# Grouped attention of a two-block kernel, turned from queries on partitions to keys on partitions

## The reference, cut to what matters

```python
def gqa_attention(q, k, v, q_norm, k_norm):
    q = apply_axial_rope(rms_norm(q.reshape(b, s, 8, 64), q_norm), tables)
    k = apply_axial_rope(rms_norm(k.reshape(b, s, 2, 64), k_norm), tables)
    ...
        scores = jnp.einsum('bqhgd,bkhd->bhgqk', q_blk, k).astype(jnp.float32) * scale
        p = jax.nn.softmax(scores, axis=-1).astype(v.dtype)
        return jnp.einsum('bhgqk,bkhd->bqhgd', p, v)
```

## Time and profile before

| | |
|---|---|
| median of 3 runs | 2565.61 us |
| the profiled execution | 2564.93 us, of which the span 2563.1 us |
| TensorE busy | 2447.2 us, 95% |
| VectorE, ScalarE, GpSimd busy | 1680.9, 1122.2, 917.6 us |
| grouped attention, first score product to last VectorE step | 1609.2 to 1819.8 us of the span |

### The profile page before, as it was taken

One profiled execution on the slowest core, in us unless ns is written; L12 is line 12 of the kernel. 1 busy time (PEld: TensorE's weight loads), 2 busy tenths in 40 slices (PEclk: granted clock), 3 DMA queues, 4 the chain that ended last, 5 costly groups with the idle time before them and its releaser, 6 DMA issues.

```text
span 2563.1 us, 33356 instructions
## 1 busy us (share of the span) xinstructions
PE 2447.2 (95%) x12995; PEld 1973.6 (77%) x12995; DVE 1680.9 (66%) x2273; ACT 1122.2 (44%) x1843; POOL 917.6 (36%) x627
## 2 busy tenths in 40 slices
PE   8999997998979999999999999899999999999997
PEld 6788885668868788888888787666687888887885
DVE  6565565777766765566687628667558665566876
ACT  5543444654444433333344534666444333333443
POOL 2332331486025655455100045311347555550000
PEclk9999998997889999999999999999999999999998
DMA  4223415353245132332854232100341332339343
GB/s 164 78 96 107 155 41 209 114 157 100 84 159 164 52 124 87 115 107 87 315 179 138 74 120 95 42 9 1 110 145 50 119 107 87 115 107 320 119 134 105
DMA packets 136284, 300.64 MB, mean 117 GB/s; under 512 B 30272, under 2 KB 30656, under 8 KB 136000
## 3 DMA queue, kind: packets, MB, share of 16 engines
q1 hardware_dynamic: 136128, 298.52, 34.5%
HBM read 220.80 MB, written 77.66 MB: 116 GB/s over the span
## 4 chain that ended last, share of the span: by engine, by line
PE 74%; DVE 12%; ACT 6%; POOL 4%; issue 2%; DMA 2%; SPq 1%; DVEq 0%; ACTq 0%; POOLq 0%
PE ps L381 20%; PE ps L383 20%; PE ps L382 20%; ACT t L397 4%; PE ps L1004 2%; PE ps L988 2%; PE ps L1024 2%; POOL t L2803 1%; DVE t L670 1%; POOL t L2811 1%; DVE t L731 1%; ACT t L1087 1%; DVE t L1138 1%; ACT t L398 1%; DVE t L1449 1%
## 5 line engine op out<-in xcount | busy, mean ns | idle before, releaser
L397 ACT ACTIVATE t<-t 128x512 fp32r<-128x512 f32 (+6 forms) x1136 | 759.6, 706 | 1118.1 <-PE ps L383 661.4
L381 PE MATMUL ps<-t 128*128 128x512 f32 (+1 forms) x2778 | 1090.0, 392 | 30.1 <-DVE t L650 9.1
L383 PE MATMUL ps<-t 128*128 128x512 f32 (+1 forms) x2778 | 1081.9, 389 | 0.0
L382 PE MATMUL ps<-t 128*128 128x512 f32 (+1 forms) x2778 | 1081.6, 389 | 0.0
L381 PEld LDWEIGHTS ps<-t 128*128 128x128 f32 x2778 | 524.2, 189 | 148.1 <-issue 17.5
L382 PEld LDWEIGHTS ps<-t 128*128 128x128 f32 x2778 | 524.3, 189 | 109.4 <-issue 2.6
L383 PEld LDWEIGHTS ps<-t 128*128 128x128 f32 x2778 | 523.8, 189 | 109.0
L2803 POOL TENSOR_TENSOR t<-t 128x512 fp32r<-128x512 f32 x280 | 416.4, 1492 | 356.5 <-ACT t L397 356.5
L484 POOL TENSOR_TENSOR t<-t 128x1024 fp32r<-128x1024 f32 x80 | 199.9, 2501 | 521.6 <-ACT t L397 521.6
L2531 DVE TENSOR_TENSOR t<-ps,t 128x512 f32<-128x512 f32 x200 | 136.7, 686 | 202.2 <-PE ps L383 202.1
L397 ACT ACTIVATE t<-ps 128x512 f32<-128x512 f32 (+5 forms) x330 | 165.9, 531 | 127.5 <-PE ps L1641 33.1
(11 more groups left out here) (202 smaller groups left out, 2356.1 us busy)
## 6 DMA issues: line engine op xcount, KB each, us to landing
t<-in_wts_dram SPq DMA_DIRECT2D x172, 512.0 KB, 3.5
t<-g_d SPq DMA_DIRECT2D x148, 256.0 KB, 2.6
g_d<-t SPq DMA_DIRECT2D x144, 256.0 KB, 2.1
t<-in_wts_dram SPq DMA_DIRECT2D x110, 256.0 KB, 4.8
t<-pj SPq DMA_DIRECT2D x39, 512.0 KB, 5.6
pj<-t SPq DMA_DIRECT2D x32, 512.0 KB, 2.7
t<-in_xT_dram SPq DMA_DIRECT2D x32, 256.0 KB, 7.0
x_d<-t SPq DMA_DIRECT2D x32, 256.0 KB, 4.2
```

Source lines behind the costliest of these rows:

```text
L381: e.matmul(out, ah, bh, start=start, stop=False, skip_group_check=goes_on)
L382: e.matmul(out, ah, bl, start=False, stop=False, skip_group_check=goes_on)
L383: return e.matmul(out, al, bh, start=False, stop=stop, skip_group_check=goes_on)
L397: return e.activation(out, in_, fn, scale=scale)
```

## The change

Grouped attention no longer uses the shared attention code. The work is 8 units u (c by two halves of 512 queries) of 8 places each, 64 places x. At a place, scores are made the other way round, 128 keys on partitions by 512 queries, so that the probabilities come out as the product with the values needs them. The transposes and their copies go.

Since the maximum over keys now runs across partitions, it is found beforehand: `pe_top` makes hi·hi scores in the old direction (128 queries by 512 keys, one pass, both heads), 64 times (y), and `dve_top` takes the negated maximum. The 16 numbers of a unit are combined, turned into two rows by 8 products with one column of weights (`rows`), copied to SBUF by ScalarE (`row_copies`), and added to every score by a product with one row of ones (K = 1, the fourth product of a bank). ScalarE then takes a plain exponential (`exps`), without a bias or a sum.

The sums of a row are made by adding the 8 tiles of probabilities of a unit: head 0 on VectorE, head 1 on GpSimd (`add_up`), and one product with ones (`sums`). The reciprocal is exp(-ln s) on ScalarE with one correcting step in two VectorE instructions.

The 8 tops of unit 0 move ahead of the stage, between the mixer's steps in `pe_mix2` and `dve_mix2`. `tops_at` says at which place each later one stands. `norms_between` puts the norm of tile 1 into places 0 to 6, one step to a place, and of tiles 2 and 3 into every second place. `pool_spread` and the stores of the mixer's result move from the start of the stage in between.

PSUM before: two slots of two banks for scores, three banks for transposes, one for the result. After: four single banks for scores, one slot of two banks for the tops, one bank for `rows` and `sums`, one for the result.

```diff
+        for s, k in before_o:
+            w.wait_ge(s, k)
...
+        def scores(x):
+            u, k = x // 8, tok[x % 8]
...
+            for i, (kk, qq) in enumerate(((kh, qh), (kh, ql), (kl, qh))):
+                for j in range(2):
+                    r = rows_of(j)
+                    e.matmul(places[j], kk[r, k], qq[r, q], start=i == 0, stop=False)
+            w.wait_ge(gq_row, u)
+            for j in range(2):
+                r = slice(64 * j, 64 * j + 1)
+                e.matmul(places[j], Q_.ones[r, :], Q_.M[u % 2][r, :], start=False, stop=True).then_inc(*gq_score.up((x, j)))
...
+    def pe_top(e, w, y):
+        u, t, k = y // 8, y % 8 // 2, halves[y % 2]
...
+            p = pe_slot(w, ("top", y), [(gq_top, y)], tops_g)
...
+            m = e.matmul(places[j], Q_.Q[u // 2 % 2][0][r, tok[4 * (u % 2) + t]], Q_.KV[0][r, k], start=True, stop=True)
...
+            m = e.tensor_reduce(Q_.tops[:, at:at + 2], top_slot.rearrange("p (j n) -> p j n", j=2), AX, MAX, negate=True)
...
+        for x in steps_g:
+            if 0 <= x < PLACES_G:
+                scores(x)
+            tops = tops_at(x)
+            for y in tops[0:1]:
+                pe_top(e, w, y)
+            between(x)
+            if 0 <= x - 2 < PLACES_G:
+                values(x - 2)
+            for y in tops[1:]:
+                pe_top(e, w, y)
+            u, at = divmod(x, 8)
+            if at == 6 and 0 <= u < UNITS_G - 1:
+                rows(u + 1)
+            if at == 2 and 0 <= u - 1 < UNITS_G:
+                sums(u - 1)
...
+        for x in steps_g:
+            for y in tops_at(x):
+                dve_top(e, w, y)
+            between(x)
+            if 0 <= x - 1 < PLACES_G:
+                add_up(e, w, x - 1, 0, gq_add)
...
+        for x in steps_g:
+            if 0 <= x - 1 < PLACES_G:
+                add_up(e, w, x - 1, 1, gq_add_p)
+            between(x)
+            if x % 8 == 2 and 0 <= x // 8 < 4:
+                pool_spread(e, w, x // 8)
```

More of the change, by code:

```diff
@@ L3211, in __init__ @@
             self.prev = None if c == "k" else c - 1 if c else "k"
+            self.places = banks if self.early else scores_g
         def take(self, w, what, until):
[L3215 to L3220, removed]
+            return [pe_slot(w, (what, self.c, h), until, self.places) for h in range(2)]
         def made(self, what):
-            if self.early:
-                return [(banks[what, self.c, h], halves[h]) for h in range(2)]
-            return [(GQ.sring[what, self.c], slice(0, L))]
+            return [(self.places[what, self.c, h], halves[h]) for h in range(2)]
     cos, sin = Q_.cs[:, 0, :], Q_.cs[:, 1, :]
-    def gqa_operands(u):
-        return Q_.Q[u.c % 2], tuple(Q_.KV), Q_.V[:].rearrange("p (t n) -> p t n", t=8), [(q_lo, u.c), (q_lo, "k"), (v_copy, 1)]
     def pe_norm(e, w, N, step):
@@ L3325, in norms_between @@
         return between
+    def pe_top(e, w, y):
+        u, t, k = y // 8, y % 8 // 2, halves[y % 2]
+        if u == 0:
+            places = [pe_slot(w, ("top", y, j), [(gq_top, y)], banks) for j in range(2)]
+        else:
+            p = pe_slot(w, ("top", y), [(gq_top, y)], tops_g)
+            places = [p[:, h] for h in halves]
+        w.wait_ge(q_hi, "k")
+        w.wait_ge(q_hi, u // 2)
+        for j in range(2):
+            r = rows_of(j)
+            m = e.matmul(places[j], Q_.Q[u // 2 % 2][0][r, tok[4 * (u % 2) + t]], Q_.KV[0][r, k], start=True, stop=True)
+        m.then_inc(*gq_max.up(y))
@@ L3327, in pe_gqa @@
     def pe_gqa(e, w):
-        GQ.sring.until[:] = [banks.until[2] + banks.until[3], banks.until[4] + banks.until[5]]
-        GQ.tring.until[:] = [banks.until[6], banks.until[7], banks.until[0]]
+        between = norms_between(e, w, pe_norm)
+        tops_g.until[0] = banks.until[2] + banks.until[3]
+        scores_g.until[:] = [banks.until[i] for i in range(4, 8)]
+        aside_g.until[0] = banks.until[0]
         before_o = banks.until[1]
[L3334 to L3341, removed]
@@ new lines, in values, with sums @@
+        def values(x):
+            u, k = divmod(x, 8)
+            if k == 0 and u:
+                w.wait_ge(gq_o, u - 1)
+            w.wait_ge(v_copy, 1)
+            V = Q_.V[:].rearrange("p (t n) -> p t n", t=8)
+            for j in range(2):
+                w.wait_ge(gq_exp, (x, j))
+            for j in range(2):
+                m = e.matmul(o_g[rows_of(j), :], V[:, k, rows_of(j)], Q_.PT[j][:, k, :], start=k == 0, stop=k == 7)
+            m.then_inc(*gq_value.up(x))
+        def sums(u):
+            p = pe_slot(w, ("sums", u), [(gq_f0, u)], aside_g)
+            for j in range(2):
+                w.wait_ge(adds[j], 8 * u + 7)
+            for j in range(2):
+                m = e.matmul(p[rows_of(j), :], ONES[:, 0:64], Q_.acc[j][u % 2][:], start=True, stop=True)
+            m.then_inc(*gq_sum.up(u))
@@ new lines, in pe_gqa @@
+        for s, k in before_o:
+            w.wait_ge(s, k)
+        w.wait_ge(z_csl, (3, 1))
+        for g in range(4):
+            m = e.matmul(o_g[:, g:g + 1], AW[:, tok[g]], M_.ny[:, g:g + 1], start=True, stop=True)
+        m.then_inc(*z_ny.up(0))
+        rows(0)
+        for x in steps_g:
[14 more added lines that the diff above has]
+                sums(u - 1)
```

171 lines of the change are left out of this document (141 added, 30 removed).

## The result

The changed kernel takes 2584.18 us (median of 4 runs, 2582.86 to 2584.95), the kernel before 2564.78 (4 runs, 2561.95 to 2565.73). The ratio is 1.008, 95% interval 1.0068 to 1.0092: 19.4 us slower, where 12.3 were forecast on the profiled run and 2578 us for the time.

What follows compares the result with a forecast made beforehand. TensorE was taken to bound the stage: start 1620, products 194.8, end 5.3 and waits 12 end it at 1832 instead of 1819.8; +12.3 gives 2577.2, plus 0.7 for the median: 2578 us, range 2550 to 2602.

Steps and rivals of the forecast that it cites:

- The place: TensorE per place: scores 0.91, one-row product 0.40, early maximum 0.40, values 1.02; 2.73 us, or 2.33 without a maximum.
- Rival 1: Going between 64 rows and 1 costs nothing, small groups 0.23 each, place 2.39: 20 us less, 2558 us; chance 0.25.
- The removed transposes are paid back: TensorE's stage products: 65 us of transposes replaced by maxima, fourth product and more shape changes; 194.8 against 193.2, +1.6.
- The start: First scores at about 1620 instead of 1609.22, behind VectorE's 16 maxima and TensorE's early maxima; bounds 1616 to 1623.
- The end: After the last score: exponentials, GpSimd's addition, sums product, ln and exp, three VectorE steps, about 7.3 us; 5.3 added.
- The waits: TensorE waiting for late VectorE through the single maxima slot, at norms and final steps: 12 us, bounds 3 and 30.
- VectorE beside GpSimd: VectorE's SBUF-only additions, 0.69 alone, wait up to 1.28 for GpSimd's addition, 0.4 on average.
- Rival 2: VectorE becomes the bound, each addition waiting out GpSimd in full: 3.15 us a place, 2583 to 2598; chance 0.15.
- Rival 3: The one-row products on TensorE don't run side by side: 15 us more, 2593; chance 0.05.
- rival 4: No change: waits of 3 us and a stage start at 1616 give 2565; chance 0.10.

Runs made afterwards that it cites:

- the kernel with 64 rows: Changed kernel with the row product reading 64 rows a head, 63 of them zeros, in place of one row; 2572.96 us, ratio to before 1.0028.

## Why the prediction held, and where its terms were off

- **The place: right.** Forecast 0.91 + 0.40 + 0.40 + 1.02, measured 0.91 + 0.43 + 0.43 + 1.01. The inference in it, that each change of shape has a price and that 64 rows to one is such a change, is shown by five kernels. Rival 1, the strongest (it is meant where the prediction speaks of the second rival's sum), needed 0.23 + 0.23 and falls; in the kernel with 64 rows its numbers come about (2.37 a place, 2.39 in the rival's sum), but the time it gives there is 2573 and not 2558.
- **The removed transposes are paid back: right.** Forecast 194.8 us of products against 193.2 before; from the places after I count 196.4 (52 x 2.76, 12 x 2.34, 2 x 0.23, 7 turned rows at 0.97, 7 sums at 0.87, 6 norm products at 1.91). The prediction had 54 places with a maximum; it is 54 maxima in 52 places, two of which have a second one, 0.4 us less.
- **The start: near in sum, wrong in its cause.** From the common mark I had +10.8 and it is +11.9; that it is so near is in part luck, as the four executions with the same start show +13.5 to +13.8. Without maxima it is 8.7 less (35.1 to 26.4), so the early maxima make most of it. VectorE sets only 2.1 us of it directly, and 1.3 ahead of the last maximum before the first scores; with the first of these waits nearly gone the time stayed.
- **The end: 4.5 us in place of 5.3.** Exponentials, sums and final steps stood in the order and at the times given.
- **The waits: the right places, a size too small.** L3358's wait for L3368 is the longest entry inside the stage. I took 12 us of waits and put the slow clock (1 to 4 us) into the range only. Waits with slow clock are 220.66 - 196.4 - 4.5 = 19.8, and by places: 3.0 at the first places (clock alone), 4.0 at norm tile 1 (forecast 5), 5.4 at tile 2 with the double maxima (2), 4.2 at tile 3 (2), 3.2 at the final steps (3). The mis-sized terms are tiles 2 and 3 and the slow clock at the first places: the double maxima at places 12 and 13 fall on norm steps, and TensorE's gap of 1.36 us there is followed by 6 us at half clock. The forecast's 12 were 5.4 less than the 17.4 before; the measured 19.8 are 2.4 more. That the single slot carries VectorE's lateness to TensorE is as forecast; that it makes the waits is not so, since they stayed, 24 us, in the kernel without maxima.
- **VectorE beside GpSimd: right in kind.** An addition of 0.69 took 1.5 to 1.8 us in 13 cases of 56, as I said (0.91 on average, where I had estimated 0.4 more than 0.69), and without GpSimd's additions the kernel is 5 to 6 us faster. Rival 2 (VectorE is the bound) does not hold for the changed kernel, though the 2584 us measured lie at the low end of its 2583 to 2598: it needed places of 3.15 us, and most are 2.76. It comes nearer in the kernels derived from it: with places of 2.37 us order took 6 of the 28 us of waits, and two additions fewer in a unit took none off the time. What exactly binds there, the port or VectorE's queue between two maxima, stays open: no run had 64 rows without GpSimd's additions.
- **Rival 3 falls** (two one-row products in one 0.43), and so does rival 4: the first scores came after the 1616 it needed, and the waits were not 3.

The sum, from the common mark: start +11.9, products +3.2, end +4.5, waits and clock +2.4, together 22.0, of which 3.5 were hidden in the profiled execution by a quicker stage ahead and 0.5 by the output projection. So the forecast of 12.3 was short by 9.7 us in what it forecast, nearly all of it waits (7.8), and by 7.1 in the time: part of its nearness is luck. The maximum as this kernel takes it costs 57 us (2584.2 to 2527.6, by the differences to before), more than the 19 that the change lost: the gain of a stage without transposes is there, and the second product, the row product and the waits for their results spend it.

## What to carry to other kernels

Count the changes of tile shape on TensorE as instructions of their own, here 0.18 us each, and give neighbours one shape even where that means multiplying zeros. Where another engine's result frees TensorE's next slot, price the wait with the slow clock that can follow it, here up to two to three times its length. Moving additions from VectorE to GpSimd gained nothing here, since the rest took longer beside them: look at what an instruction takes beside its neighbour, not at what it takes alone. And where an engine is late, removing the place where the lateness shows does not remove it.

## What the runs showed of the hardware that I had not expected

- A product with one row costs as much in going over from 64 rows as one with 128 rows: 0.18 us at 2.4 GHz, whatever the order.
- After gaps of 1.36 us, or of 1.87 and 1.55 with little between, the granted clock was at 0.51 to 0.52 for 6 us with TensorE busy, 1.2 GHz, and at 1.00 in the window after that. Thus 3.4 us of waits cost 6.8, and the gap of 1.36 about 4. Not every wait is followed so: behind the same wait of 2.1 us at the start the clock stayed full in the changed kernel's execution and was at half for 3.4 us in four others.
- Executions of one kernel lie up to 10 us apart (2568.8 to 2578.9 with 64 rows), and their granted clock goes along (0.972 and 0.975 in the two shortest, 0.968 to 0.970 in the four longest); from kernel to kernel the trace's times from a common mark agree with the medians' differences to 4.5 us or better.
